# An attention bias table moved from the router's stage to the first projections

## The chip, the core and the metric

The kernel runs on one core of one Trainium2 chip. The metric is the device time of one execution in microseconds (us), as the median of several runs.

## What is computed

Two transformer blocks over 256 tokens of width 1024, all in f32. The first block projects x with one wide matrix and runs four token mixers on the result: A (RWKV-7), B (HGRN2), C (mLSTM) and D (RG-LRU). Their outputs are gated, merged, projected and added to x (layer norm 1); then come a mixture of 32 experts with the top 4 per token, and a gated embedding ("ple"). The second block has attention in three dilated windows and a pooling mixer. Its attention adds a relative position bias:

```python
dist = BLOCK + i - j
bucket = t5_bucket(jnp.clip(dist, 0, n_back) * dil)
bias = jnp.transpose(bias_g[bucket].astype(jnp.float32), (2, 0, 1))
logits = jnp.where(mask[None, :, None], logits + bias[None, None], -jnp.inf)
```

There are 24 heads (3 groups of 8), and the bias of a head depends on the distance of query and key alone.

## The kernel before

The kernel is written by hand, one instruction stream for each engine, with semaphores between them. SBUF is one tensor, `arena`, cut by offsets into named rooms, so that rooms of different stages overlap; PSUM is four banks `proj` and four banks `small`. Each product that goes through a `small` bank has a name in the list SMALL (L130 to L154), and the n-th uses bank n % 4: TensorE waits until VectorE has emptied the product four places ahead (`small`, L611), and VectorE takes them in the same order (`full`, L1581). PROJ and the `proj` banks work alike, with ScalarE emptying them (`out`, L1340).

SyncE (L500) streams the weights. The list UNITS (L111) has one entry for each 2 MB of weights, in the order in which TensorE uses them: "D xr", "D gate", "C q", "C k", "C if" (32 KB), "C v", "C o", "B f", ... They go through a ring of three rooms, so the load of unit n is issued when unit n-3 has been used (L504, L510). Behind the last of them SyncE loads the weights of expert 0 (L515 to L518, six units), then runs a loop over the experts in which each unit is loaded again as soon as TensorE has used it (L521 to L529), and then UNITS2 for the second block.

TensorE (L599) transposes x (L658), multiplies the first half of "D xr" (L667), transposes the packed vectors (L670), and goes on with "D xr", "D gate", "C q" (`ones_channels`, matmul at L627), the gates of D (L681), "C k", "C if" (L688), "C v" (`ones_tokens`, L637), "C o" and so on. The mixers' own chains come between projections. The end of the first block is `mixed` (L1039), `x1_turned` (L1049), `logits` (L1058), `ada_rows` (L820), `ada` (L828), then "ple" (L1102) and "pp" (L1143); the expert loop has L1176 (gate and up) and L1208 (down).

VectorE ends that stage with `residual` (L2002), `centred` (L1991 to L1993) and `normed` (L1997) for each of the two token tiles. Between the two calls for the second tile ScalarE computes a reciprocal root (`rsqrt`, L1407 and L1408). `normed` signals `x1_done`, for which `x1_turned` on TensorE waits.

The bias table is made of three small inputs: `rel_bias_2` (32 buckets x 24 heads), `hot` (32 x 384, each column the bucket of one distance) and `mask` (24 x 384). GpSimd loads them (L575 to L577) after the second merge. TensorE multiplies RELB by HOT behind the last `mixed` (L1066, L1067), VectorE adds the mask between `centred` and `normed` of the second tile (L2021 to L2023), and ScalarE stores the 24 x 384 result 128 times over into DRAM (L1470, L1471: 3072 rows of 1536 bytes, 4.7 MB). SyncE reads it back with a slanted access pattern (L535 to L538), which turns it into the bias for every query, in the second block. The buffers RELB, HOT, BM and TAB lie among the router's and the modulation's small tensors (L362 to L368).

At the start GpSimd loads two gate biases (L548, L549), clears WX and WAD (L550, L551), loads the blocks of D's gates into them (L555), and three matrices of A (L557 to L559). VectorE copies XT (L1607) and the vectors (L1608), then computes a small chain of lru_lambda together with ScalarE (L1616 to L1625, L1368, L1370), then the convolutions (L1630, L1632). ScalarE empties "D xr", "D gate" and "C q" and then does the sigmoids of D's gates (L1376, L1377); much later, when the last of B's projections is out, it computes the sigmoid of qB into the room tB (L1418).

## Time and profile before

| | before |
|---|---|
| median of 3 runs | 1945.26 us (1944.66 to 1947.16) |
| profiled execution, its own time | 1947.88 us |
| its span, first to last instruction | 1945.7 us |
| TensorE busy | 1835.1 us (94%) |
| VectorE busy | 553.8 us (28%) |
| ScalarE busy | 237.2 us (12%) |
| GpSimd busy | 43.9 us (2%) |
| mean granted TensorE clock | 0.975 of full speed |
| DMA | 537.69 MB, mean 276 GB/s |

The span in 40 equal slices of 48.6 us; a digit is a share in tenths, 9 is 90% or more:

```profile
PE   8999998899999999999999999999999979999998
PEld 7688886699865344333333333333333327768984
DVE  3543486555234211111111111111111130014412
ACT  0322122000100001100101101101101111011100
POOL 1000000130000000000000000000000000000000
PEclk9999998899898999999999999999999989999999
DMA  7443342512138899999999999999999975532331
GB/s 258 147 156 124 105 140 87 189 72 90 47 122 299 351 422 428 428 428 428 429 428 428 428 428 428 429 428 429 427 429 427 429 287 195 165 130 87 103 135 60
```

The first 12 slices are the projections and mixers of the first block up to layer norm 1, the 13th and 14th are router, "ple" and the first expert, the 15th to the 32nd the expert loop, and the rest the second block. PE is TensorE's matmuls, PEld its weight loads, which overlap them. In the loop the DMA rate stands at 427 to 429 GB/s.

### The profile page before, as it was taken

How to read it: one execution, taken by the hardware profiler on the slowest of the kernel's cores; microseconds unless marked ns; L12 is line 12 of the kernel's file. 1: busy time of each engine (PE TensorE's matmuls, PEld its weight loads, DVE VectorE, ACT ScalarE, POOL GpSimd, SP SyncE). 2: the span in 40 equal slices, each digit the busy share in tenths (PEclk: the TensorE clock that was granted, in tenths of full speed). 3: DMA queues.
4: the chain of work that ended last, by engine and by line, in shares of the span. 5: the costliest groups of instructions: out<-in, count | busy, mean ns of one | idle time of the engine just before them, and what ended most of it. 6: DMA issues, size and time to landing. Idle time of an engine off the chain costs nothing. (4 is left out here: it accounts for less than half of the span.)

```text
span 1945.7 us, 21418 instructions
## 1 busy us (share of the span) xinstructions
PE 1835.1 (94%) x8829; PEld 1074.9 (55%) x8829; DVE 553.8 (28%) x1037; ACT 237.2 (12%) x379; POOL 43.9 (2%) x39
## 2 busy tenths in 40 slices
PE   8999998899999999999999999999999979999998
PEld 7688886699865344333333333333333327768984
DVE  3543486555234211111111111111111130014412
ACT  0322122000100001100101101101101111011100
POOL 1000000130000000000000000000000000000000
PEclk9999998899898999999999999999999989999999
DMA  7443342512138899999999999999999975532331
GB/s 258 147 156 124 105 140 87 189 72 90 47 122 299 351 422 428 428 428 428 429 428 428 428 428 428 429 428 429 427 429 427 429 287 195 165 130 87 103 135 60
DMA packets 94139, 537.69 MB, mean 276 GB/s; under 512 B 5763, under 2 KB 15277, under 8 KB 69385
## 3 DMA queue, kind: packets, MB, share of 16 engines
q1 hardware_dynamic: 88960, 527.53, 67.4%
q10 hardware_dynamic: 3464, 4.85, 0.9%
q0 software_dynamic: 1664, 4.58, 0.8%
q8 instruction: 38, 0.62, 0.1%
q14 instruction: 13, 0.10, 0.0%
HBM read 531.18 MB, written 5.77 MB: 276 GB/s over the span
## 5 line engine op out<-in xcount | busy, mean ns | idle before, releaser
L1176 PE MATMUL small<-arena 128*64 128x512 f32 x2048 | 459.7, 597 | 44.2 <-DMA arena<-in_expert_w_gu 44.2
L1176 PEld LDWEIGHTS small<-arena 128*64 128x64 f32 x2048 | 160.0, 137 | 338.3 <-issue 248.7
L1208 PE MATMUL small<-arena 128*64 128x512 f32 x1024 | 226.8, 594 | 4.6
L2119 DVE TENSOR_SCALAR arena<-small 128x512 f32<-128x512 f32 x32 | 22.1, 692 | 721.7 <-PE small L1183 721.7
L627 PE MATMUL proj<-arena 128*128 128x256 f32 x960 | 211.5, 381 | 0.0
L627 PEld LDWEIGHTS proj<-arena 128*128 128x128 f32 x960 | 182.6, 191 | 25.7 <-issue 1.0
L1229 PE MATMUL proj<-arena 128*128 128x256 f32 x768 | 167.5, 379 | 0.0
L1229 PEld LDWEIGHTS proj<-arena 128*128 128x128 f32 x768 | 145.4, 190 | 20.3 <-issue 1.0
L1208 PEld LDWEIGHTS small<-arena 128*64 128x64 f32 x1024 | 84.7, 137 | 124.6 <-issue 124.6
L1347 ACT ACTIVATE arena<-proj 128x512 f32<-128x512 f32 (+1 forms) x76 | 45.3, 597 | 542.5 <-PE proj L885 168.3
L1485 ACT ACTIVATE arena<-arena 128x512 f32<-128x512 f32 x32 | 20.2, 630 | 548.1 <-DVE arena L2119 548.1
L1158 PE MATMUL proj<-arena 64*128 64x512 f32 x264 | 65.6, 615 | 0.7 <-ACTq L1495 0.7
L1123 PE MATMUL small<-arena 128*64 128x512 f32 x264 | 63.9, 605 | 0.0
L1238 PE MATMUL proj<-arena 128*128 128x512 f32 x128 | 59.9, 626 | 3.9 <-DVE arena L2145 3.9
L885 PE MATMUL proj<-arena 128*128 128x256 f32 x256 | 63.0, 402 | 0.0
L885 PEld LDWEIGHTS proj<-arena 128*128 128x128 f32 x256 | 50.6, 203 | 7.5
L2176 DVE TENSOR_TENSOR arena<-proj,arena 128x512 f32<-128x512 f32 (+2 forms) x24 | 13.4, 558 | 124.2 <-PE proj L1272 123.7
L648 PE MATMUL small<-arena 128*128 128x256 f32 x192 | 45.5, 401 | 3.4 <-DVE arena L1964 3.4
L1158 PEld LDWEIGHTS proj<-arena 64*128 64x128 f32 x264 | 22.7, 186 | 43.1 <-issue 41.5
L1493 ACT ACTIVATE arena<-small 128x512 f32<-128x512 f32 x32 | 19.1, 597 | 212.3 <-PE small L1208 212.3
L1238 PEld LDWEIGHTS proj<-arena 128*128 128x128 f32 x128 | 25.6, 203 | 34.7 <-issue 30.1
L648 PEld LDWEIGHTS small<-arena 128*128 128x128 f32 x192 | 38.6, 202 | 9.5 <-DVE arena L1964 3.6
(445 smaller groups left out, 1634.2 us busy)
## 6 DMA issues: line engine op xcount, KB each, us to landing
arena<-in_expert_w_gu SPq DMA_DIRECT2D x128, 2048.0 KB, 24.7
arena<-in_expert_w_down SPq DMA_DIRECT2D x64, 2048.0 KB, 20.4
arena<-in_w_in_first SPq DMA_DIRECT2D x20, 2048.0 KB, 7.8
arena<-in_w_in SPq DMA_DIRECT2D x16, 2048.0 KB, 9.1
arena<-in_w_ada SPq DMA_DIRECT2D x6, 2048.0 KB, 7.9
arena<-in_w_branch SPq DMA_DIRECT2D x4, 2048.0 KB, 7.8
arena<-in_w_out SPq DMA_DIRECT2D x4, 2048.0 KB, 8.1
bias_rows<-arena ACTq DMA_DIRECT2D x1, 4608.0 KB
```

The lines of the kernel that those rows point to most:

```text
L627: mm = pe.matmul(ps[:, m * T:m * T + T], w[:, k, (2 * b + m) * P:(2 * b + m + 1) * P], XT[:, k, :], start=k == 0, stop=k == KD - 1)
L648: mm = pe.matmul(ps[:, m * T:m * T + T], w[:, k, (2 * i + m) * P:(2 * i + m + 1) * P], YT[b][:, k, :], start=k == 0, stop=k == KW - 1)
L885: mm = pe.matmul(ps[:, m * T:m * T + T], w[:, k, quarter * P:quarter * P + P], XT[:, k, :], start=k == 0, stop=k == KD - 1)
L1123: mm = pe.matmul(bank[CAP * half:CAP * half + CAP, :], PICK[:, j, :], x1[:, j, half * W:half * W + W], start=j == 0, stop=j == 1, skip_gro ...
L1158: mm = pe.matmul(acc_bank[2 * j + half][:, :], PTW[lo:lo + CAP, j * P:j * P + P], YSB[lo:lo + CAP, :], start=False, stop=False, skip_group ...
L1176: mm = pe.matmul(bank[CAP * half:CAP * half + CAP, :], XG[:, k % 4, k // 4, :], w[:, k % 2, n * D + half * W:n * D + half * W + W], start= ...
L1208: mm = pe.matmul(y_bank[CAP * half:CAP * half + CAP, :], HM[:, m, u, :], w[:, m, half * W:half * W + W], start=u == 0 and m == 0, stop=u = ...
L1229: mm = pe.matmul(ps[:, m * T:m * T + T], w[:, k, (2 * b + m) * P:(2 * b + m + 1) * P], HT[:, k, :], start=k == 0, stop=k == KD - 1)
L1238: mm = pe.matmul(ps[:, :], HT[:, k, j * P:j * P + P], w[:, k, :], start=k == 0, stop=k == KD - 1)
L1347: act.activation(dst, v, func).then_inc(sig("proj_out"), 1)
L1485: act.activation(SGH, GH, ACT.Sigmoid, scale=1.702).then_inc(sig("sig_ready"), 1)
L2119: TS(GH, gate_bank[:, :], 7.0, None, ALU.min).then_inc(sig("g_ready"), 1)
```

## The change

The three loads move to the start of GpSimd's stream; the matmul follows the transposition of the vectors on TensorE, and in SMALL "bias" now stands behind "vectors"; the add follows the copy of the vectors on VectorE; the store is issued by ScalarE behind the evictions of "C q". RELB, HOT and TAB lie in the room that branch B later uses as tB (HIGH + 9728), the mask is loaded into TAB itself and added in place, and ScalarE waits for the store before it writes tB. The small statistics of layer norm 2 and later move to another offset.

```diff
--- before.py
+++ after.py
@@ -127,7 +127,7 @@
             ([f"L {h + 1} {i}" for i in range(3)] if h < 7 else []) + [f"{('Z', 'U', 'ZP', 'g2a')[h // 2]} {h % 2}"]]
          + ["g2a 2", "g2a 3"] + [f"g2p {i}" for i in range(4)])
 
-SMALL = ([f"x {i}" for i in range(4)] + ["vectors"]
+SMALL = ([f"x {i}" for i in range(4)] + ["vectors", "bias"]
          + ["D gx 0", "D gx 1", "D ga 0", "D ga 1"]
          + ["C row 0", "C row 1", "C col"] + [f"C S {h}" for h in range(4)]
          + ["C num 0", "C num 1", "C den", "C yT 0", "C yT 1"]
@@ -146,7 +146,7 @@
          + ["A S 0", "A U 1 0", "A U 1 1", "A S 1", "A Y 0", "A Y 1", "A U 2 0", "A U 2 1", "A S 2", "A U 3 0", "A U 3 1"]
          + ["A Y 2", "A Y 3", "A yT 0", "A yT 1"]
          + [f"Wb A {i}" for i in range(4)] + ["mix 0", "mix 1", "mix 2", "x1 0 0", "x1 0 1", "mix 3"]
-         + ["bias", "logits 0", "ada rows 4", "x1 1 0", "x1 1 1", "logits 1", "pT", "ada rows 5", "ada 4", "ada 5", "gate8"]
+         + ["logits 0", "ada rows 4", "x1 1 0", "x1 1 1", "logits 1", "pT", "ada rows 5", "ada 4", "ada 5", "gate8"]
          + ["ple 0", "gateB 0", "gateB 1", "ple 1", "gateT", "rank", "ple 2", "ple 3", "picked", "pp 0", "pp 1", "xg", "pp 2", "pp 3"]
          + ["h 0", "h 1"]
          + [f"{n} {h}" + s_ for h in range(HEADS) for n, s_ in (("T", " 0"), ("T", " 1"), ("T", " 2"), ("O", ""))]
@@ -283,6 +283,9 @@
         tB2 = room(at, KW, T); at += 1024
         stB = room(at, 2, 8); at += 16
         fB0 = tB2
+        RELB = room(HIGH + 9728, 24)[0:32]
+        HOT = room(HIGH + 9728 + 24, BKT)[0:32]
+        TAB = room(HIGH + 9728 + 24 + BKT, BKT)[0:24]
         assert at <= HIGH + 3 * UNIT
 
 
@@ -359,14 +362,10 @@
         PV2 = room(at, 40); at += 40
         MODT = room(at, 24); at += 24
         G8 = room(at, P)[0:8]; at += P
-        RELB = room(at, 24)[0:32]; at += 24
-        HOT = room(at, BKT)[0:32]; at += BKT
         CB = room(at, KD, 32); at += KD * 32
         SEL = room(at, 1); at += 1
         assert at <= LOW - 3 * 1024
-        BM = room(at, BKT)[0:24]; at += BKT
-        TAB = room(at, BKT)[0:24]; at += BKT
-        assert at <= LOW - 2 * 1024
+        at = LOW - 2 * 1024 - 64
         st2 = room(at, 2, 12); mv2 = room(at + 24, 2, 2); rs2 = room(at + 28, 2); ss2 = room(at + 30, 2)
         rs3 = room(at + 32, 2); ss3 = room(at + 60, 2, 2)
         mod_a = room(at + 36, 8); den = room(at + 44, 2, 4); nmax = room(at + 52, 2, 4)
@@ -547,6 +546,8 @@
         def _(pool):
             pool.dma_start(ifb[0:4, 0:1], ins["mlstm_i_bias"].rearrange("a b -> b a")).then_inc(sig("ifb_loaded"), 16)
             pool.dma_start(ifb[0:4, 1:2], ins["mlstm_f_bias"].rearrange("a b -> b a")).then_inc(sig("ifb_loaded"), 16)
+            for dst, src in ((RELB, ins["rel_bias_2"]), (HOT, consts["hot"]), (TAB, consts["mask"])):
+                pool.dma_start(dst, src).then_inc(sig("table_loaded"), 16)
             pool.memset(WX, 0.0).then_inc(sig("wx_zero"), 1)
             pool.memset(WAD, 0.0).then_inc(sig("wx_zero"), 1)
             pool.wait_ge(sig("wx_zero"), 2)
@@ -572,9 +573,6 @@
                     pool.wait_ge(sig("small_full"), small_no(f"A X{l - 1} 3") + 1)
                 pool.tensor_tensor(NTm, NT, along(c("level", l * P, l * P + P), 16), ALU.mult).then_inc(sig("NTm_ready"), 1)
 
-            pool.wait_ge(sig("merged"), 2)
-            for dst, src in ((RELB, ins["rel_bias_2"]), (HOT, consts["hot"]), (BM, consts["mask"])):
-                pool.dma_start(dst, src).then_inc(sig("table_loaded"), 16)
             pool.wait_ge(sig("A_states_done"), 1)
             pool.wait_ge(sig("small_full"), small_no("A Y 3") + 1)
             pool.dma_start(bcg, ins["ln1_g"][0].partition_broadcast(P)).then_inc(sig("ln1_loaded"), 16)
@@ -668,6 +666,8 @@
             mm.then_inc(sig("proj_full"), 1)
             pe.wait_ge(sig("prow_loaded"), 16 * len(VEC))
             pe.transpose(small("vectors")[:, 0:NVEC], PROW[0:NVEC, :], ident[0:NVEC, 0:NVEC]).then_inc(sig("small_full"), 1)
+            pe.wait_ge(sig("table_loaded"), 48)
+            pe.matmul(small("bias")[0:24, 0:BKT], RELB, HOT, start=True, stop=True).then_inc(sig("small_full"), 1)
             ones_channels("D xr", (1,))
             ones_channels("D gate")
             ones_channels("C q")
@@ -1063,8 +1063,6 @@
             mixed(1, 0)
             x1_turned(0)
             mixed(1, 1)
-            pe.wait_ge(sig("table_loaded"), 48)
-            pe.matmul(small("bias")[0:24, 0:BKT], RELB, HOT, start=True, stop=True).then_inc(sig("small_full"), 1)
             logits(0)
             ada_rows(4)
             x1_turned(1)
@@ -1371,6 +1369,9 @@
             channels("D xr", xr[:, :, 3:])
             channels("D gate", lgate)
             channels("C q", cz[:, 0:4, 3:])
+            act.wait_ge(sig("table_done"), 1)
+            act.dma_start(scratch.rearrange("p h c -> h p c"), along(TAB, P)).then_inc(sig("table_stored"), 16)
+
 
             act.wait_ge(sig("D_gates"), 1)
             do(act.activation(gx, gx, ACT.Sigmoid), "D_sig")
@@ -1415,6 +1416,7 @@
                 out(f"B i {j}", vB[:, j, :])
             channels("B g", gB)
             act.wait_ge(sig("proj_out"), proj_no("B g 1") + 1)
+            act.wait_ge(sig("table_stored"), 16)
             do(act.activation(tB, qB, ACT.Sigmoid))
             do(act.activation(kB, fB0, ACT.Sigmoid, scale=-1.0))
             do(act.activation(eB, gB, ACT.Sigmoid), "B_sig")
@@ -1467,9 +1469,6 @@
             log_and_exp()
             for j in range(TT):
                 rsqrt(rs1[:, j:j + 1], "ln1_var", "ln1_rstd", j + 1)
-            act.wait_ge(sig("table_done"), 1)
-            act.dma_start(scratch.rearrange("p h c -> h p c"), along(TAB, P)).then_inc(sig("table_stored"), 16)
-
             act.wait_ge(sig("logits_ready"), 1)
             do(act.activation(ex, ex, ACT.Exp), "router_exp")
             for i in range(4):
@@ -1606,6 +1605,9 @@
             for g in range(4):
                 do(dve.tensor_copy(XT[:, 2 * g:2 * g + 2, :], tiles(full(f"x {g}"))), "small_out")
             do(dve.tensor_copy(PV[:, 0:NVEC], full("vectors")[:, 0:NVEC]), "small_out")
+            dve.wait_ge(sig("table_loaded"), 48)
+            do(TTn(TAB, full("bias")[0:24, 0:BKT], TAB, ALU.add), "small_out")
+            dve.nop().then_inc(sig("table_done"), 1)
 
 
             do(dve.memset(xr[:, :, 0:3], 0.0))
@@ -2018,9 +2020,6 @@
             x1_turned(0)
             residual(1, 1)
             centred(mixv, st1, mv1, rs1, bcg, 1, "ln1_var")
-            dve.wait_ge(sig("table_loaded"), 48)
-            do(TTn(TAB, full("bias")[0:24, 0:BKT], BM, ALU.add), "small_out")
-            dve.nop().then_inc(sig("table_done"), 1)
             normed(x1, mixv, rs1, bcb, 1, "ln1_rstd", "x1_done")
             logits(0)
             ada_rows(4)
```

## Rows read from the trace of the kernel before

**Rows 1.** Waits of TensorE, 660 to 1640 us: us in total, times, longest.
```profile
PE small L1176 <- DMA arena<-in_expert_w_gu: 44.2, 51, 1.3
```

**Rows 2.** Busy time by stretch: us, PE PEld DVE ACT POOL, PEclk, DMA share, GB/s.
```profile
660.00:670.00 10.00, 10.00 (x40) 3.13 (x38) 0.57 (x3) 0.00 (x0) 0.00 (x0) 0.79 0.75 275
670.00:680.00 10.00, 10.00 (x50) 2.92 (x46) 2.77 (x5) 0.63 (x1) 0.00 (x0) 1.00 1.02 436
```

**Rows 3.** Time line of SyncE: start us, us, what.
```profile
665.52 0.35 SPq L529 DMA_DIRECT2D arena<-in_expert_w_gu  x1
```

**Rows 4.** Busy time by stretch again, two of the first 60 of 10 us.
```profile
20.00:30.00 10.00, 10.00 (x49) 8.76 (x48) 3.21 (x15) 1.61 (x4) 0.00 (x0) 1.00 1.06 409
200.00:210.00 10.00, 10.00 (x52) 8.85 (x51) 2.70 (x7) 1.88 (x2) 0.00 (x0) 1.00 0.59 211
```

**Rows 5.** Waits of TensorE, 0 to 600 us.
```profile
PE small L828 <- DVE arena L1814: 4.0, 1, 4.0
```

**Rows 6.** Time line around the old place of the bias table.
```profile
591.47 0.82 PE L1067 MATMUL small<-arena 32*24 32x384 f32 x2
592.22 1.97 PE L1058 MATMUL small<-arena 128*128 128x32 f32 x16
593.83 0.20 ACT L1408 ACTIVATE arena<-arena 128x1 f32<-128x1 f32 x1
594.86 0.55 DVE L2022 TENSOR_TENSOR arena<-small,arena 24x384 f32<-24x384 f32 x1
595.55 0.33 ACTq L1471 DMA_DIRECT2D bias_rows<-arena  x1
595.56 1.28 DVE L1997 SCALAR_TENSOR_TENSOR arena<-arena 128x1024 f32<-128x1024 f32 x1 [0.16 <-DVE arena L2022]
596.90 1.09 PE L1049 MATMUL small<-arena 128*128 128x128 f32 x8 [0.85 <-DVE arena L1997]
```

**Rows 7.** Busy time by stretch, two of 5 us behind the old place.
```profile
600.00:605.00 5.00, 5.00 (x26) 3.77 (x29) 1.76 (x8) 0.00 (x0) 0.00 (x0) 0.50 0.73 199
610.00:615.00 5.00, 4.68 (x12) 2.79 (x12) 0.61 (x3) 0.00 (x0) 0.00 (x0) 0.50 0.96 235
```

**Rows 8.** DMA issues, us to landing last, three stretches: 604:612, 620:622, 0:120.
```profile
arena<-in_ple_gate_w SPq DMA_DIRECT2D x1, 2048.0 KB, 18.2
...
arena<-in_expert_w_gu SPq DMA_DIRECT2D x1, 2048.0 KB, 27.0
...
arena<-in_rwkv_g POOLq DMA_DIRECT2D x1, 256.0 KB, 9.1
```

**Rows 9.** Waits of TensorE, 590 to 700 us.
```profile
PE small L828 <- DVE arena L1814: 1.7, 1, 1.7
```

**Rows 10.** Time line around the new place of the matmul.
```profile
20.53 0.27 PE L670 MATMUL small<-arena 126*128 126x126 f32 x1
...
27.75 0.60 ACT L1347 ACTIVATE arena<-proj 128x512 f32<-128x512 f32 x1 [4.62 <-PE proj L627]
```

**Rows 11.** Time line of the first 12 us, three rows.
```profile
1.91 0.54 POOL L549 DMA_DIRECT2D arena<-in_mlstm_f_bias  x1
...
10.30 0.69 DVE L1607 COPY arena<-small 128x512 f32<-128x512 f32 x1 [0.16 <-PE small L658]
11.39 2.04 PE L667 MATMUL proj<-arena 128*128 128x256 f32 x4 [1.19 <-DMA arena<-in_w_in_first]
```

**Rows 12.** Time line of 55 to 94 us, around the store's new place.
```profile
55.37 0.37 SPq L510 DMA_DIRECT2D arena<-in_w_in_first  x1
...
59.68 1.06 ACT L1376 ACTIVATE arena<-arena 128x1024 f32<-128x1024 f32 x1 [2.41 <-DVEq L1645]
...
72.63 0.37 SPq L510 DMA_DIRECT2D arena<-in_w_in_first  x1
...
79.53 14.00 PE L637 MATMUL proj<-arena 128*128 128x512 f32 x32
93.37 27.79 PE L627 MATMUL proj<-arena 128*128 128x256 f32 x128
```

## The prediction

> **What bounds the kernel now.** I read the waits of TensorE over the expert loop first, then the stretches around the loop's start, then the time lines of the two places that the change touches. In the expert loop TensorE's one large wait is for the gate and up weights, 44.2 us in 51 waits [rows 1], and from 670 us on the DMA engines are busy throughout (share 1.02, 436 GB/s, [rows 2]). So the loop is bound by the stream of weights. The stream's start is not: between 660 and 670 us the DMA share is only 0.75 [rows 2], because expert 0 fills the ring ahead of time and the first reload waits until TensorE has used a unit of it. SyncE issues that reload at 665.5 us [rows 3]. Whatever moves TensorE before 665.5 us moves the stream, and with it the end, by as much; what moves a transfer alone before that moves nothing, unless TensorE comes to wait for it.
>
> Before 665.5 us TensorE is the chain. From 20 to 210 us it is busy without a gap (first and last of 19 stretches of 10 us, all with 10.00 us busy, [rows 4]). From there to 590 us it waits now and then for VectorE or GpSimd, 4.0 us in the longest wait [rows 5], and those chains start from TensorE's own products, so that a delay of TensorE early on passes through them.
>
> **The old place, TensorE and VectorE.** The table's matmul starts at 591.47 us and the router's first logits matmul at 592.22: it takes 0.75 us of TensorE's issue [rows 6]. But TensorE waits a little later, 0.85 us, for L1997, the last step of the second layer norm tile, before it transposes that tile (L1049) [rows 6]. So what counts is when L1997 is done. On VectorE the table's add L2022 stands ahead of it: the add starts at 594.86 us, L1997 at 595.56. ScalarE's reciprocal root was ready at 593.83 + 0.20 = 594.03 [rows 6], so without the add L1997 can start where the add did, 595.56 - 594.86 = **0.70 us earlier**. What is late next is again VectorE, with the copies of x1, and then the second logits: the same order as before, with TensorE 0.75 us earlier in front of it, so all of it moves by 0.70. After that the top-4 chain on VectorE, the row copy for "ada 5", TensorE's waits at L828 for it (1.7 us, [rows 9]) and the "ple" units follow one another without slack up to 665.5 us. Term: **-0.70 us**. Ends: 0, if something that I don't see holds the copies back; and -1.05, because from 600 to 605 us the granted clock is at 0.50, the level of 1.2 GHz [rows 7], and 0.70 us more of the second logits would run at 2.4 GHz before it falls, which saves half of that, 0.35.
>
> **The old place, transfers.** The store (L1471) is an issue of 0.33 us on ScalarE [rows 6], which then has nothing to do until the router's exponential: 0. Its traffic is not small. With it the DMA share is 0.73 at only 199 GB/s between 600 and 605 us [rows 7], the second "ple" unit needs 18.2 us to land and an expert unit 27.0 us [rows 8]. But that "ple" unit is issued when "ada 4" is used, near 608 us, and wanted some 23 us later; expert 0 is wanted only behind "pp", the experts' biases and more; in the list of TensorE's waits between 590 and 700 us the longest is for VectorE, 1.7 us, and none is for a DMA [rows 9]. So taking the traffic away is worth **0**, under the cover of TensorE's own work. GpSimd's three loads, which stand between merge C and a wait for branch A's states, keep nobody waiting: 0.
>
> **The new place, TensorE.** The matmul goes in behind the transposition of the vectors (L670) and ahead of the second half of "D xr" (L627), where TensorE does nothing but issue. It costs its issue time. The nearest row is the same matmul in the old place, 0.75 us from its start to the next one's [rows 6]. Ends: 0.27 us, which the transposition of 126 columns takes [rows 10], and 0.82 us, the busy time of the table's own [rows 6]. I take **+0.75 us**. All of it lasts, for TensorE is busy without a gap for 190 us more. The Trainium skill, page "TensorE: Matmul & The Clock Gate", section "Back-to-back issue gap", gives N/2.4 + 2.5 ns for one pass at the full clock; four passes of 384 columns would be 0.65 us (an estimate, the number of passes is mine), and by it the sum below would be 0.10 us lower.
>
> **The new place, the loads.** GpSimd issues the three loads behind the two of the gate biases, of which the second takes 0.54 us and ends at 2.45 us [rows 11]; loads of its queue land in 9.1 us at most [rows 8]. So the last, issued by 4.1, is there by some 13 us, and TensorE asks at 20.8: 0. On GpSimd the two memsets, the loads of lru_wx and lru_wa and those behind them move back by 3 x 0.54 = 1.6 us; the first of them is wanted behind "C q 1", near 55 us: 0. One transfer does hold TensorE here, the first half of "D xr", 1.19 us until 11.39 [rows 11]. The three loads are 90 KB; ahead of it, at the 199 GB/s of the slowest stretch shown [rows 7], they are 0.45 us. On the other side 1.6 us of the lru traffic now come later, and TensorE could begin up to 0.3 us sooner, after VectorE's last copy (10.30 + 0.69, [rows 11]). I take 0, with -0.3 and +0.45 as ends.
>
> **The new place, VectorE and ScalarE.** VectorE waits for the matmul (done near 21.7 us) and adds for 0.55 us, so the lru_lambda chain behind it on both engines and ScalarE's first eviction come some 1.3 us later. ScalarE is idle for 4.62 us before its second eviction at 27.75 [rows 10], VectorE's convolutions wait for that eviction, and the bank of the first is wanted again only by "C q 0", near 41 us: 0. The store is issued behind "C q 1", where ScalarE then waits 2.41 us for VectorE [rows 12]: 0.33 us, hidden. The wait for the store ahead of the sigmoid of tB stands five units of weights further on, more than 90 us: 0. The traffic now meets the loads of "C v" (issued 55.37 us, wanted 79.53) and "C o" (issued 72.63, wanted 93.37) [rows 12]. With the 18.2 us of the "ple" unit they land at 73.6 and 90.8, both in time: 0.
>
> **Sum.** +0.75 - 0.70 = **+0.05 us**, between -1.1 (0.27 - 0.3 - 1.05) and +1.3 (0.82 + 0.45 - 0). The profiled execution took 1947.88 us, 2.2 us around its span of 1945.7; it lies 2.6 us above the median of the three runs shown, 1945.26 (1944.66 to 1947.16). The difference is put on the median: **1945.3 us**.
>
> **Rivals.**
> - The store stalls TensorE (0.04). Its traffic moves from under work that had no use for the DMA to where each unit is wanted soon. It decides at "C o": if that load takes more than 93.37 - 72.63 = 20.7 us, TensorE stands. With the slowest landing under the store, 27.0 us [rows 8], the wait is 6.3 us and the time 1951.6. Against it: the unit of the 27.0 us had others ahead of it in its queue, "C o" has none.
> - The clock (0.13). The stretches 600 to 605 and 610 to 615 us lie wholly at 0.50 [rows 7]. Such a low stretch is some 6.5 us long, so one more or one less is worth up to half, 3.2 us. The work there is thin: short waits, matmuls of 32 columns. If the shift of 0.7 us lets one go, 1942.0 (0.08); if it brings one, 1948.5 (0.05). By the Trainium skill, the same page, section "The HAM clock gate (the "warmup" mystery)", the gate follows how busy the engine has been of late, on a schedule that does not start with the kernel; by that rule a matmul taken out of a thin stretch speaks against this change, which is the 1948.5; the trace agrees in that both stretches follow waits of TensorE. For a shift that does nothing: four executions of the kernel lie within 3.2 us, each begun at another moment.
> - Half of the change is swallowed (0.06): one of TensorE's waits between 210 and 590 us takes up the 0.75 us, and the 0.70 stay: 1944.6. Against it: those waits hang on TensorE's own products.
>
> **How the numbers follow.** My forecast has 0.77. A measurement of this kernel can tell about 0.2% from no change, 3.9 us: below 1941.4 or above 1949.2. Faster, 0.05: a low stretch gone together with the lower end of the other terms, or two gone. Slower, 0.05: the store's 0.04 and 0.01 of the clock. Same, 0.90. The range takes in one low stretch either way and the ends of the sum, 1942.0 to 1948.5.
>
> **What would show it.** Right: the table's matmul near 21 us and the next projection 0.75 us behind; no DMA wait of TensorE for "C v" or "C o", with the DMA share near 1 behind 56 us; L1997's successor right behind L1993; the expert units ahead of the loop landing faster, to nobody's use; the first reload within 1 us of 665.5. Wrong: a DMA wait of TensorE between 76 and 110 us, ScalarE held at the store's issue, another number of low stretches before 665 us.

## The result, and the profile of the changed kernel

| | before | after |
|---|---|---|
| median, 20 runs each on one chip | 1944.6 us (1942.18 to 1947.33) | 1948.24 us (1939.38 to 1951.19) |
| ratio, 95% interval | | 1.0015 (1.0008 to 1.0021) |
| profiled execution / its span | 1947.88 / 1945.7 us | 1947.88 / 1945.7 us |

The change costs 0.15%, 2.9 us by the ratio. That is inside the 0.2% that was called no change, though the end of the interval, 1.0021, passes that bound. The forecast was 1945.3 us, with a range from 1942.0 to 1948.5; the median lies 0.3 us under the upper end. The two profiled executions took the same time to the hundredth, so the cost is not to be found by setting one profile against the other. It is found over all runs, further down. The profiles do show what became of each step. The page first, in the order of busy times, slices of TensorE, granted clock, DMA and rate:

```profile
PE 1835.3 (94%) x8829; PEld 1077.5 (55%) x8829; DVE 553.7 (28%) x1037; ACT 237.2 (12%) x379; POOL 44.0 (2%) x39
...
PE   8999998899998999999999999999999979999998
...
PEclk9999999799898999999999999999999999999999
DMA  7743333521236799999999999999999975542331
GB/s 260 238 157 111 111 120 107 184 87 53 79 125 253 295 420 428 429 428 429 428 429 428 429 428 429 428 429 428 429 428 429 428 290 199 167 130 87 103 134 61
```

The store's 4.7 MB now lie in the second slice (238 GB/s; it was 147), and the 13th and 14th carry less (253 and 295; they were 299 and 351). The clock's low digit has moved as well.

**The first microseconds**, time line of GpSimd, VectorE and TensorE (start, duration, engine, line, operation; in brackets the idle time before it and what ended it):

```profile
2.44 0.53 POOL L550 DMA_DIRECT2D arena<-in_rel_bias  x1
...
3.47 0.52 POOL L550 DMA_DIRECT2D arena<-shape_mask  x1
...
10.05 0.69 DVE L1606 COPY arena<-small 128x512 f32<-128x512 f32 x1 [0.16 <-PE small L656]
...
10.80 9.46 PE L665 MATMUL proj<-arena 128*128 128x256 f32 x32 [0.85 <-DVE arena L1606]
...
20.09 0.27 PE L668 MATMUL small<-arena 126*128 126x126 f32 x1
...
20.30 0.82 PE L670 MATMUL small<-arena 32*24 32x384 f32 x2
...
21.05 10.20 PE L625 MATMUL proj<-arena 128*128 128x256 f32 x46
21.25 0.55 DVE L1609 TENSOR_TENSOR arena<-small,arena 24x384 f32<-24x384 f32 x1 [0.49 <-PE small L670]
...
28.26 0.60 ACT L1345 ACTIVATE arena<-proj 128x512 f32<-128x512 f32 x1 [4.42 <-PE proj L625]
```

TensorE starts "D xr" at 10.80 us instead of 11.39 [rows 11], and behind VectorE's copy instead of a transfer. The table's matmul takes 0.75 us of issue, 20.30 to 21.05, as in the old place. VectorE's add is there at 21.25, and ScalarE still has 4.42 us to spare ahead of its second eviction.

**The store and the units that it meets**, time line of ScalarE, SyncE and TensorE, then the list of DMA issues (KB each, us to landing) for "C v" and "C o":

```profile
55.89 0.37 ACTq L1373 DMA_DIRECT2D bias_rows<-arena  x1
...
60.19 1.06 ACT L1377 ACTIVATE arena<-arena 128x1024 f32<-128x1024 f32 x1 [2.41 <-DVEq L1647]
...
73.14 0.37 SPq L509 DMA_DIRECT2D arena<-in_w_in_first  x1
...
80.05 14.00 PE L635 MATMUL proj<-arena 128*128 128x512 f32 x32
93.88 6.42 PE L625 MATMUL proj<-arena 128*128 128x256 f32 x29
```

```profile
arena<-in_w_in_first SPq DMA_DIRECT2D x1, 2048.0 KB, 12.9
...
arena<-in_w_in_first SPq DMA_DIRECT2D x1, 2048.0 KB, 19.2
```

"C o" was issued at 73.14 us, landed 19.2 us later at 92.3, and was wanted at 93.88: a margin of 1.5 us. In a4_store_late, the experiment below that has no store here, the same two loads landed in 7.7 and 7.9 us. Neither unit makes TensorE wait; the rows of their matmuls, at 80.05 and 93.88, have no idle time before them.

**The old place**, time line of TensorE and VectorE, and TensorE's waits from 590 to 700 us (idle us, times, mean):

```profile
595.75 0.69 DVE L2004 SCALAR_TENSOR_TENSOR arena<-arena,small 128x512 f32<-128x512 f32 x1 [4.87 <-PE small L1039]
...
598.96 1.28 DVE L1999 SCALAR_TENSOR_TENSOR arena<-arena 128x1024 f32<-128x1024 f32 x1
...
600.30 0.88 PE L1049 MATMUL small<-arena 128*128 128x128 f32 x6 [1.10 <-DVE arena L1999]
```

```profile
PE small L828 <- DVE arena L1816: 2.0, 1, 2.0
...
PE small L1049 <- DVE arena L1999: 1.1, 1, 1.1
```

No wait is for a DMA, and the longest is the one for VectorE at L828, 2.0 us, before 1.7 [rows 9]. From the residual L2004 to L1999, the last step of the layer norm, it is 598.96 - 595.75 = 3.21 us. Before, it was 3.90 (L2002 at 591.66, L1997 at 595.56). The add's 0.69 us have gone from VectorE's path. But this profile reaches the place 4.1 us late: the residual is at 595.75 instead of 591.66.

**Where the 4.1 us were lost, and got back.** The stretches of the changed kernel (length, TensorE busy, weight load, VectorE, ScalarE, GpSimd, granted clock, DMA share, GB/s), and those of the kernel before:

```profile
120.00:130.00 10.00, 10.00 (x41) 8.20 (x40) 3.68 (x10) 2.58 (x3) 0.00 (x0) 0.83 0.60 210
220.00:230.00 10.00, 6.18 (x29) 5.63 (x28) 5.59 (x9) 1.06 (x1) 1.53 (x3) 0.68 0.61 212
655.00:660.00 5.00, 5.00 (x13) 2.07 (x12) 3.14 (x5) 0.00 (x0) 0.00 (x0) 1.00 0.38 98
660.00:665.00 5.00, 5.00 (x21) 1.67 (x21) 2.51 (x6) 0.00 (x0) 1.08 (x2) 1.00 0.90 374
```

```profile
120.00:130.00 10.00, 10.00 (x50) 8.48 (x49) 3.68 (x10) 3.10 (x3) 0.00 (x0) 1.00 0.61 210
220.00:230.00 10.00, 7.59 (x43) 6.92 (x44) 7.35 (x12) 1.06 (x1) 0.00 (x0) 1.00 0.41 153
655.00:660.00 5.00, 5.00 (x12) 1.48 (x12) 3.45 (x5) 0.00 (x0) 1.07 (x2) 0.75 0.88 305
660.00:665.00 5.00, 5.00 (x16) 1.44 (x14) 0.57 (x3) 0.00 (x0) 0.00 (x0) 0.57 0.80 324
```

In the clock records the changed kernel has two low stretches, of 3.4 us from 124.9 and of 6.8 us from 223.9, where the kernel before has none. The kernel before has one of 6.8 us from 657.5, ahead of the loop, where this profile of the changed kernel has none. So SyncE's issues, 4.1 us late at the first "ple" unit (595.67 us instead of 591.57), are level again at the first reload of the loop, 665.62 us against 665.52 [rows 3]:

```profile
665.62 0.35 SPq L528 DMA_DIRECT2D arena<-in_expert_w_gu  x1
```

From the reload on the time is the same (665.62 to the end: 1280.08 us, before 1280.18). The loop's wait for weights is 44.5 us; it was 44.2 [rows 1].

Two single profiles do not show that the edit made the stretches at 125 and 224 us. The kernel of the experiment a3_late_removed, below, is the kernel before up to 590 us, and its profile has them too:

```profile
120.00:130.00 10.00, 10.00 (x42) 8.14 (x41) 3.80 (x11) 3.48 (x4) 0.00 (x0) 0.83 0.60 210
220.00:230.00 10.00, 6.31 (x24) 5.81 (x25) 5.83 (x9) 1.06 (x1) 0.76 (x2) 0.66 0.53 198
```

**All executions.** Each execution comes with its span and its mean granted clock c. The low level is 1.2 GHz, 0.50 of the full 2.4. So span x (1 - c) is the time lost to it if TensorE sets the pace throughout, and span x c is what the program would then take at full clock; call it the work. The clock is given to three digits, up to 1 us in one execution, but the means are good to some 0.5 us. Over 103 executions of the kernel before (those beside the experiments below) and all others, means with standard errors:

| kernel | work, us | lost to low clock, us | executions with c of 0.974 or less |
|---|---|---|---|
| before | 1897.65 ± 0.17 | 44.9 ± 0.2 | 0 of 103 |
| after | 1896.7 ± 0.4 | 48.7 ± 0.8 | 10 of 20 |
| a1_loads_only | 1896.6 ± 0.5 | 44.3 | 0 of 11 |
| a2_early_doubled | 1898.15 ± 0.4 | 45.4 | 0 of 11 |
| a3_late_removed | 1896.7 ± 0.4 | 45.4 | 0 of 11 |
| a4_store_late | 1896.1 ± 0.3 | 49.4 ± 1.1 | 7 of 11 |
| b1_spread_after | 1899.8 ± 0.5 | 46.2 | 0 of 11 |
| b2_spread_before | 1901.5 ± 0.4 | 43.4 | 0 of 12 |
| b3_more_work | 1897.6 ± 0.3 | 46.7 | 0 of 11 |
| b4_fill | 1903.4 ± 0.3 | 40.6 | 0 of 11 |
| c1_split_after | 1899.2 ± 0.4 | 45.0 | 0 of 12 |
| c2_split_loads_only | 1898.2 ± 0.35 | 42.9 | 0 of 12 |
| c3_loads_behind | 1896.6 ± 0.5 | 50.0 ± 0.9 | 8 of 12 |
| c4_before_more | 1898.0 ± 0.3 | 43.6 | 0 of 11 |

By this split the change makes the work 0.9 us less and the loss 3.8 us more, together the 2.9 us of the ratio. Half of its executions lie lower in the clock than any of the kernel before: those ten took 1949.7 us in the mean, the other ten 1945.4. The profiled one, c = 0.976, is of the second kind.

The split is rough, because low time in which TensorE waits costs nothing. At the end of the loop before's profile has 17.1 us of low clock (from 1592.8 us), the changed kernel's 13.7 (from 1596.1). The split books 1.7 us of loss for that, and the two profiles take the same time from the reload to the end within 0.1 us; TensorE stands idle there until 1600.07 us, for 9.4 us at a stretch, and the 3.4 us more lie in that idle time. Within the kernels (259 executions, each against the mean of its kernel) 0.001 less of c goes with 1.35 us more span, not 1.95, and the rounding of c explains only some 0.1 of the difference. So, as an estimate, about a quarter of what is booked as loss is none, and the column of work is too small by as much. By this estimate the 3.8 us of loss cost 2.9, all of the change's price, and its work is level. Differences of less than 1 us in the column of work are not to be read.

The bound of 0.974 is no sharp one either. Counted at 0.975 or less it is 5 of 103 for before, 11 of 20 for after, 7 of 11 for a4, 11 of 12 for c3, 4 of 11 for b1, 3 of 12 for c1, 1 of 11 each for a1, a2 and a3, and none for the rest.

### The profile page after: what moved, and what is told of

Read it like the earlier page. It is cut to its first block and busy times, and to the rows that moved or that the text cites. A ratio compares the mean times of both kernels' runs of the same rounds, so it can differ in the third digit from the quotient of the medians.

```text
span 1945.7 us, 21420 instructions
## 1 busy us (share of the span) xinstructions
PE 1835.3 (94%) x8829; PEld 1077.5 (55%) x8829; DVE 553.7 (28%) x1037; ACT 237.2 (12%) x379; POOL 44.0 (2%) x39
## 5 line engine op out<-in xcount | busy, mean ns | idle before, releaser
L1174 PE MATMUL small<-arena 128*64 128x512 f32 x2048 | 457.3, 595 | 44.5 <-DMA arena<-in_expert_w_gu 44.5
L1156 PE MATMUL proj<-arena 64*128 64x512 f32 x264 | 65.6, 615 | 0.7 <-ACTq L1494 0.7
L1121 PE MATMUL small<-arena 128*64 128x512 f32 x264 | 63.9, 605 | 0.0
L885 PE MATMUL proj<-arena 128*128 128x256 f32 x256 | 62.4, 400 | 0.0
```

The costliest lines, as they stand in the source:

```text
L885: mm = pe.matmul(ps[:, m * T:m * T + T], w[:, k, quarter * P:quarter * P + P], XT[:, k, :], start=k == 0, stop=k == KD - 1)
L1121: mm = pe.matmul(bank[CAP * half:CAP * half + CAP, :], PICK[:, j, :], x1[:, j, half * W:half * W + W], start=j == 0, stop=j == 1, skip_gro ...
L1156: mm = pe.matmul(acc_bank[2 * j + half][:, :], PTW[lo:lo + CAP, j * P:j * P + P], YSB[lo:lo + CAP, :], start=False, stop=False, skip_group ...
L1174: mm = pe.matmul(bank[CAP * half:CAP * half + CAP, :], XG[:, k % 4, k // 4, :], w[:, k % 2, n * D + half * W:n * D + half * W + W], start= ...
```

## The experiments

Each was timed against the kernel before on one chip. Two accounts of the extra time were tried against each other: that it is the clock, falling once more in some executions because of where TensorE's work stands, and that it is real work or waiting that the moved loads, matmul or store bring.

| kernel | median, us (range), runs | ratio to before (95%) |
|---|---|---|
| a1_loads_only | 1942.67 (1941.26 to 1945.29), 11 | 0.9992 (0.9983 to 1.0001) |
| a2_early_doubled | 1945.73 (1941.86 to 1948.26), 11 | 1.0005 (0.9996 to 1.0014) |
| a3_late_removed | 1943.95 (1941.81 to 1946.35), 11 | 0.9995 (0.9986 to 1.0004) |
| a4_store_late | 1948.49 (1941.45 to 1951.16), 11 | 1.0016 (1.0004 to 1.0027) |
| b1_spread_after | 1948.73 (1942.88 to 1951.3), 11 | 1.0014 (1.0005 to 1.0023) |
| b2_spread_before | 1947.7 (1942.7 to 1950.46), 12 | 1.0012 (1.0003 to 1.0021) |
| b3_more_work | 1946.26 (1945.09 to 1947.97), 11 | 1.0008 (1.0 to 1.0017) |
| b4_fill | 1946.7 (1942.53 to 1948.66), 11 | 1.0008 (0.9999 to 1.0017) |
| c1_split_after | 1946.94 (1939.54 to 1950.43), 12 | 1.0008 (0.9997 to 1.0019) |
| c2_split_loads_only | 1942.68 (1940.88 to 1946.33), 12 | 0.9996 (0.9987 to 1.0004) |
| c3_loads_behind | 1948.94 (1943.43 to 1950.87), 12 | 1.0023 (1.0014 to 1.0031) |
| c4_before_more | 1942.98 (1941.66 to 1946.9), 11 | 0.9997 (0.9988 to 1.0006) |

Medians of before beside them: 1944.69 (33 runs, a), 1944.51 (35, b), 1944.46 (35, c). The three groups ran on three chips, and the changed kernel was not timed again beside them. Where a run is set against the changed kernel's 20, the comparison goes by way of the kernel before, whose medians agree within 0.25 us.

### The parts alone

**a1_loads_only**: the kernel before, and the three loads early as well, into rooms of their own.

```diff
+            for dst, src in ((RELE, ins["rel_bias_2"]), (HOTE, consts["hot"]), (TABE, consts["mask"])):
+                pool.dma_start(dst, src).then_inc(sig("early_loaded"), 16)
             pool.memset(WX, 0.0).then_inc(sig("wx_zero"), 1)
```

> The kernel before, with the three small loads issued early a second time into branch B's room, where nobody reads them; matmul, add and store stay at the old place. In the changed kernel TensorE's first projection began 0.43 us sooner than before. Theory LOADS (the reordered GpSimd queue does that): the same here, and the time within 1 us of before. Theory CLOCK (the +3 us of the change is low-clock time that a small shift of TensorE's early work brings): a shift of -0.4 us can by itself move the time by 1 to 3 us, and the time follows the mean granted clock of each run. Theory STORE (the store's traffic among the early loads costs the time): no change against before.

It came out 2.0 us under the kernel before, more than an account without gain allowed, though the interval of the ratio still reaches 1.0001. By the table it is work, -1.0 us, and 0.6 us less loss, neither of them clear by itself. The profile shows the transfer's wait gone:

```profile
11.01 8.95 PE L672 MATMUL proj<-arena 128*128 128x256 f32 x32 [0.85 <-DVE arena L1613]
```

Instead of waiting for the DMA until 11.39 us [rows 11], TensorE starts at 11.01, behind VectorE. In all nine profiles with the small loads at the front of GpSimd's stream TensorE starts between 10.62 and 11.04 us, in the five without between 11.39 and 11.84. That the larger lru loads, pushed back by them, are what "D xr" competed with is the reading that fits; it was not measured by itself.

**a2_early_doubled**: a1 with the early matmul and add as well; the old place keeps its own.

```diff
-SMALL = ([f"x {i}" for i in range(4)] + ["vectors"]
+SMALL = ([f"x {i}" for i in range(4)] + ["vectors", "bias0"]
...
+            pe.wait_ge(sig("early_loaded"), 48)
+            pe.matmul(small("bias0")[0:24, 0:BKT], RELE, HOTE, start=True, stop=True).then_inc(sig("small_full"), 1)
...
+            dve.wait_ge(sig("early_loaded"), 48)
+            do(TTn(TABE, full("bias0")[0:24, 0:BKT], TABE, ALU.add), "small_out")
```

> The kernel before, with loads, matmul and add at the new place into a room that nobody reads, and the whole old place kept, the store too. Theory CLOCK: the early shift alone brings the loss, so +0.75 us of work and about 2 to 3 us of low clock, 3 to 4 us over before. Theory STORE: +0.75 us only. Theory SUM (my prediction's terms and nothing else): +0.75 us, at most 1.

The work is 1.5 ± 0.6 us above a1's, where 0.75 was the price of the matmul: the right sign, and the size is off by little more than one error. No execution has the low clock of the changed kernel. The account by the clock, 3 to 4 us over before from the early part alone, missed: by the ratio it is 1.0 us.

**a3_late_removed**: the kernel before without the late matmul and add; the store writes the mask alone.

```diff
-            pe.wait_ge(sig("table_loaded"), 48)
-            pe.matmul(small("bias")[0:24, 0:BKT], RELB, HOT, start=True, stop=True).then_inc(sig("small_full"), 1)
...
-            do(TTn(TAB, full("bias")[0:24, 0:BKT], BM, ALU.add), "small_out")
-            dve.nop().then_inc(sig("table_done"), 1)
...
-            act.dma_start(scratch.rearrange("p h c -> h p c"), along(TAB, P)).then_inc(sig("table_stored"), 16)
+            act.dma_start(scratch.rearrange("p h c -> h p c"), along(BM, P)).then_inc(sig("table_stored"), 16)
```

> The kernel before, without the table's matmul and add at the old place, nothing at the new one; the store stays at the old place and stores the mask alone. The product of the relative bias is left out. Theory SUM: -0.7 us. Theory CLOCK: -0.7 us plus or minus one low stretch behind the place, -4 to +3, with the start of the kernel as before. Theory STORE: -0.7 us.

Work 0.9 ± 0.5 us less; the term was 0.70. Again no execution at 0.974 or less. So neither part alone brings the loss.

**a4_store_late**: the changed kernel with a store of the same size, of the mask alone, put back behind the layer norm.

```diff
-            act.wait_ge(sig("table_done"), 1)
-            act.dma_start(scratch.rearrange("p h c -> h p c"), along(TAB, P)).then_inc(sig("table_stored"), 16)
...
+            act.wait_ge(sig("mask_loaded"), 16)
+            act.dma_start(scratch.rearrange("p h c -> h p c"), along(BM, P)).then_inc(sig("table_stored"), 16)
             act.wait_ge(sig("logits_ready"), 1)
```

> The changed kernel with the store put back behind the layer norm, from a room into which the mask alone is loaded; the matmul and the add stay early. The product is left out of what is stored. Theory STORE: the loss of 3 us goes, the time is that of before within 1 us. Theory CLOCK: it stays, 2 to 4 us over before.

1948.49 us, like the changed kernel, with work, loss and share of executions (7 of 11 against 10 of 20) the same within their errors. The store's place is not the cause. Its profile also shows the extra fall. Time line of TensorE around the start of the loop, and the stretches there:

```profile
656.90 4.37 PE L1151 MATMUL proj<-arena 32*128 32x512 f32 x8
661.21 16.62 PE L1177 MATMUL small<-arena 128*64 128x512 f32 x64
```

```profile
655.00:660.00 5.00, 5.00 (x12) 1.97 (x11) 3.55 (x3) 0.00 (x0) 0.00 (x0) 0.98 0.59 184
660.00:665.00 5.00, 5.00 (x12) 1.24 (x12) 1.32 (x6) 0.00 (x0) 1.08 (x2) 0.50 0.94 395
665.00:670.00 5.00, 5.00 (x22) 1.52 (x20) 0.00 (x0) 0.00 (x0) 0.00 (x0) 0.84 0.67 198
```

TensorE is busy without a gap, from 656.90 us on with eight matmuls (32 rows, 512 columns) that set up the experts' biases, and the clock is low for 6.8 us from 660.1. Expert 0's 64 matmuls then take 16.62 us. In the changed kernel's profile, without a low stretch there, they take 13.95:

```profile
658.09 3.69 PE L1148 MATMUL proj<-arena 32*128 32x512 f32 x8
661.72 13.95 PE L1174 MATMUL small<-arena 128*64 128x512 f32 x64
```

This profiled execution is the only one of the fourteen kernels' that has c at 0.974 or less (0.973). So it is the one view of which stretch a slower execution has more. Granted clock of stretches of 20 us, where the profiles differ most, and the low time between 100 and 700 us worked out from them (twice the missing share of each stretch):

| profile | 120 | 220 | 640 | 660 | low, us |
|---|---|---|---|---|---|
| before | 1.00 | 1.00 | 0.94 | 0.89 | 68.4 |
| after | 0.91 | 0.83 | 1.00 | 1.00 | 68.8 |
| a2, a3, b1, b3, c1, c3 | 0.91 | 0.83 | 1.00 | 1.00 | 68.4 to 68.8 |
| a4 | 0.91 | 0.83 | 0.99 | 0.83 | 76.0 |
| b2 | 1.00 | 0.83 | 1.00 | 1.00 | 65.6 |
| a1, c4 | 0.91 | 0.91 | 1.00 | 1.00 | 62.4 |
| c2 | 1.00 | 0.88 | 1.00 | 1.00 | 65.2 |
| b4 | 0.91 | 0.91 | 1.00 | 1.00 | 52.0 |

(The stretches from 160, 300 to 380, 500 to 560 and 600 us are low in part in nearly all of them, and are in the last column too.) Before's profile has the low stretch ahead of the loop and not those at 125 and 224 us; most others have these and not that; a4's has both, and 7.2 to 7.6 us more low time than the profiles of before and after. Half of it would be 3.6 to 3.8 us; the block and expert 0's matmuls together took (4.37 - 3.69) + (16.62 - 13.95) = 3.35 us longer than in the changed kernel's profile. At the end of the loop a4's has 3.4 us of low time more as well (17.1 us from 1595.4), as before's has, which is part of its low c. The stretch of 3.4 us at 123 to 125 us and one at 222 to 224 stand in the profile of c4 too, whose kernel is the kernel before up to some 640 us. So where the stretches lie differs between profiles for another reason than the edit.

### The block of 32 rows, and more work

**b1_spread_after** and **b2_spread_before**: in the changed kernel and in that of before, the block is cut up, one of its four products behind each product of "pp".

```diff
                 mm.then_inc(sig("small_full"), 1)
+                pe.matmul(acc_bank[2 * j + half][:, :], GTT[:, j * P:j * P + P], BD[:, half * W:half * W + W], start=True, stop=False, skip_group_check=True)
...
-            for j in range(TT):
-                for half in range(2):
-                    pe.matmul(acc_bank[2 * j + half][:, :], GTT[:, j * P:j * P + P], BD[:, half * W:half * W + W], start=True, stop=False, skip_group_check=True)
```

> The changed kernel with the four matmuls of 32 rows that start the accumulators ahead of the expert loop (the line with GTT and BD) no longer in one block behind the last pp product but one behind each of the four. Same work. In profiles of the kernel before and of the changed kernel with the store put back, the granted clock falls to 0.50 at the end of that block and stays there for 6.8 us into the first expert; in those of the changed kernel itself and of the doubled early part it doesn't, and these executions are some 3 us shorter. Theory CLOCK: the fall at that place goes for good, the median is 2 to 3 us under the changed kernel's 1948.2 and the spread over the executions smaller. Theory WORK (the change adds 3 us of waits or work): no difference against the changed kernel, 1948.

> The same edit on the kernel before. Theory CLOCK: before had the fall at that place in few executions only, so little is won, 0 to 1 us, and the gap between the two kernels shrinks from 3.6 us to 1 us or less. Theory WORK: the gap stays at 3 us.

The loss is 46.2 ± 0.8 us in b1 against 48.7 ± 0.8, and no execution of 11 is at 0.974 or less, though four are at 0.975. But the edit costs work: 3.1 us in b1 and 3.9 in b2. The account by the clock, which expected 2 to 3 us under the changed kernel, missed. One piece of it can be read in b1's time line:

```profile
661.79 1.12 PE L1144 MATMUL proj<-arena 32*128 32x512 f32 x2
663.88 13.95 PE L1171 MATMUL small<-arena 128*64 128x512 f32 x64 [0.97 <-issue]
```

From L1121 at 648.63 us to the loop's first matmul it takes 15.2 us, where the changed kernel takes 13.0 (648.69 to 661.72). The medians, 1948.73 and 1947.7, are 1.0 us apart instead of the 3.6 of the kernels that they were made of. The edit takes away most of the difference between them, but it brings both near the level of the slower one.

**b3_more_work** puts one matmul of 128 rows and 512 columns, used by nobody, in front of the "picked" gather of the changed kernel; **c4_before_more** does the same to the kernel before.

```diff
+            pe.wait_ge(sig("proj_out"), proj_no("G A 3") + 1)
+            pe.matmul(acc_bank[0][:, :], ident, CO[:, 0:W], start=True, stop=True)
             pe.wait_ge(sig("pick_ready"), 1)
```

> The changed kernel with 0.86 us of extra TensorE work, one matmul of 128x512 that nobody reads, ahead of the first expert's gather, where TensorE is the chain. Theory WORK: 0.9 us slower than the changed kernel, 1949.1. Theory CLOCK: the place of the 32-row block moves by 0.86 us and with it how often the clock falls there; the doubled early part, which reaches this place some 0.7 us later than the changed kernel, was faster than it by 2.5 us, so here 1945.5 to 1947, with more work in less time.

> The kernel before with the 0.86 us of extra TensorE work ahead of the first expert's gather that took 2 us off the changed kernel. Theory WORK: +0.9 us against before, 1945.4. Theory CLOCK: here the fall ahead of the loop was rare and the shift can only make it more frequent or leave it, +0.9 to +3 us.

With more work the changed kernel did not get slower: 0.9 us more of it, 2.1 us less lost, 1946.26 us, and in the mean 1.1 ± 0.8 us less time. All eleven executions have c = 0.976, and they spread over 2.9 us instead of 11.8. An account by work alone asks for 0.9 us more and is off by 2.0 ± 0.8. But c4 missed: with the same matmul the kernel before came out at 1942.98, 1.5 us under its own median instead of above it (0.6 by the ratio, whose interval takes in 1), with 1.3 ± 0.6 us less lost and the work hardly up (+0.35). The loss moves by 1 to 2 us, each time some two errors, through edits whose own price is less than 1.

**b4_fill**: b1 with five such matmuls of 256 or 512 columns put into TensorE's thin stretches at the logits and the modulation.

```diff
+            def busy(n, cols):
+                for _ in range(n):
+                    pe.matmul(acc_bank[0][:, 0:cols], ident, CO[:, 0:cols], start=True, stop=True)
...
             ada_rows(4)
+            busy(1, 256)
             x1_turned(1)
+            busy(1, 512)
             logits(1)
...
             ada_rows(5)
+            busy(3, 512)
             ada(4)
```

> The changed kernel with the spread accumulator matmuls and with matmuls that nobody reads in three waits of TensorE behind the layer norm: 256 columns ahead of the transpositions of the second tile, 512 ahead of its logits, 3 x 512 ahead of ada 4. Theory CLOCK: with TensorE busy through these waits one or both of the low stretches between 599 and 617 us go, each worth up to 3.4 us: 1940 to 1944. Theory WORK: nothing gained or up to 1 us lost against the spread version.

The stretches of b4, and of the changed kernel:

```profile
600.00:610.00 10.00, 8.89 (x43) 4.61 (x36) 5.80 (x23) 0.26 (x1) 0.00 (x0) 0.87 0.38 134
610.00:620.00 10.00, 10.00 (x34) 5.15 (x33) 2.07 (x3) 1.91 (x2) 0.00 (x0) 0.96 1.04 425
```

```profile
600.00:610.00 10.00, 8.14 (x44) 5.59 (x44) 5.38 (x19) 0.26 (x1) 0.00 (x0) 0.66 0.27 104
610.00:620.00 10.00, 7.71 (x27) 4.86 (x24) 3.66 (x13) 0.00 (x0) 0.00 (x0) 0.66 0.78 281
```

Where TensorE stands less, the clock stays up: 0.87 and 0.96 instead of 0.66 and 0.66. Behind the layer norm one stretch of 3.4 us is left of two of 6.8. Over all runs 8.1 us less are lost than in the changed kernel, and 6.7 us more work done: 1946.7 us. Against b1, which has the same spread block, it is 5.5 us less lost for 3.6 us more work. The expectation by the clock, 1940 to 1944, missed by what the fillers and the spread block cost.

**c1_split_after** and **c2_split_loads_only** look for a split without b1's price: of the block's four products, two go behind "ple 2" and "ple 3" and two stay (c1 from the changed kernel, c2 from a1).

```diff
+                    if half == 1:
+                        if j == 0:
+                            pe.wait_ge(sig("small_out"), small_no("gateT") + 1)
+                        started(0, j)
...
-            for j in range(TT):
-                for half in range(2):
-                    pe.matmul(acc_bank[2 * j + half][:, :], GTT[:, j * P:j * P + P], BD[:, half * W:half * W + W], start=True, stop=False, skip_group_check=True)
+            for half in range(2):
+                started(1, half)
```

> The changed kernel with two of the four 32-row matmuls that start the accumulators moved up, one behind each of the products ple 2 and ple 3, so that the block ahead of the expert loop is half as long and still covers VectorE's work on the last pp product (the spread version lost 1.0 us there and about as much between its matmuls). Theory CLOCK: no fall of the clock ahead of the loop and no more than 0.3 us of cost, 1944.5 to 1946.5, that is 2 to 3.5 us under the changed kernel. Theory WORK: 1948 to 1949.

> The version with the early loads alone, which was the fastest so far (1942.67, 2 us under before), with the same split. Theory CLOCK: it had the fall ahead of the loop in few executions, so -0.5 to +0.3 us, 1942 to 1943, below both kernels. Theory WORK: 1942.7 to 1943.

c1 loses 3.7 ± 1.2 us less than the changed kernel and works 2.5 us more: 1946.94, a little above what was expected. c2 is at 1942.68, no better than a1, since the split again costs what it saves.

**c3_loads_behind**: the changed kernel with the three loads behind those of lru_wx and lru_wa.

```diff
-            for dst, src in ((RELB, ins["rel_bias_2"]), (HOT, consts["hot"]), (TAB, consts["mask"])):
-                pool.dma_start(dst, src).then_inc(sig("table_loaded"), 16)
             pool.memset(WX, 0.0).then_inc(sig("wx_zero"), 1)
...
+            for dst, src in ((RELB, ins["rel_bias_2"]), (HOT, consts["hot"]), (TAB, consts["mask"])):
+                pool.dma_start(dst, src).then_inc(sig("table_loaded"), 16)
             pool.dma_start(WA2[0:64, :], ins["rwkv_w2"][0])
```

> The changed kernel with GpSimd's three loads behind those of lru_wx and lru_wa instead of ahead of them. If the changed order of GpSimd's loads is what let TensorE begin at 11.0 instead of 11.4 us, it begins at 11.4 or later here, waiting for the first half of D xr. Theory SUM: 0.4 to 0.7 us over the changed kernel, 1948.9. Theory CLOCK: the work without the low clock is 0.4 to 0.7 us more than the changed kernel's, the time itself anywhere between 1944.5 and 1950, by the share of executions with low stretches.

```profile
11.84 1.39 PE L665 MATMUL proj<-arena 128*128 128x256 f32 x4 [2.25 <-DMA arena<-in_w_in_first]
```

The transfer's wait is back, 2.25 us of it, and TensorE starts at 11.84 instead of 10.80. So where these loads stand among GpSimd's does set the start. The work over all runs does not show the 1.0 us, though (1896.6 against 1896.7, each ± 0.5). The extra loss stays: 8 of 12 executions at 0.974 or less, 1948.94 us. Part of it has another source here: this profile's clock records have a low stretch of 3.4 us from 12.7 us, beside the wait for the transfer, that no other profile's records show. It counts for 1.7 us of the 50.0, and 48.3 would still be 3.4 above before.

## Why the prediction was right, and where it was not

"No change" was right, and the path and most terms were as worked out. That the time lies in the stated range is luck in part: the forecast was 2.9 us too low, nearly all of it the clock, and the range held because its upper end was the rival of one low stretch more, which had been given 0.05.

**The bound**: right. In the profiles of all 14 kernels the end lies 1279.3 to 1282.6 us behind the first reload, wherever between 659.2 and 667.8 us that is. The first four expert units landed sooner (median 14.5 us instead of 23.5) and served nobody. That this profile's reload at 665.62 us was within 1 us of 665.5, one of the signs of being right, is chance: those of a1 and c4 have it at 661.4 and 661.1.

**New place, TensorE** (+0.75): 20.30 to 21.05 us, +0.75. The estimate from the Trainium skill, page "TensorE: Matmul & The Clock Gate", section "Back-to-back issue gap", 0.65, is not borne out; its number of passes was a guess.

**Old place** (-0.70): the path from the residual to L1999 is shorter by 0.69 us. TensorE then waits 1.10 us for L1999, before 0.85, and the next steps follow as before.

**The start** (0, between -0.3 and +0.45): it measured 11.39 - 10.80 = 0.59 us of gain in the profiles, past the lower end. The two effects that were weighed against each other were the right ones, but the order of the loads outweighs the 90 KB by more than was thought. a1 and c3 show the step by itself, the one taking the wait away and the other bringing it back, and so do the ranges over all profiles, 10.62 to 11.04 us and 11.39 to 11.84; part of the gain in the changed kernel is VectorE's last copy, at 10.05 instead of 10.30 us. These three terms give 0.75 - 0.70 - 0.59 = -0.54 us; the mean of the work says -0.9 ± 0.4, or about nothing once a quarter of the loss is booked back. Neither is clear of the forecast's +0.05.

**The store** (0, a rival of 0.04): right, by 1.5 us. "C o" took 19.2 us of the 20.7 that it had, more than the 18.2 by which the place was judged, and "C v" 12.9. a4 shows no difference in time by the store's place. The sign "DMA share near 1 behind 56 us" did not come as stated: the share was 0.95, 0.76, 0.70 and 0.93 in the four stretches of 5 us from 60 us. With more than another 1.5 us on "C o" the store would have held TensorE up.

**The clock**: here the working failed. The forecast gave "a shift that does nothing" nearly all the weight, on the ground that four executions of the kernel before lie within 3.2 us, and the rival of one low stretch more, 1948.5 us, 0.05. That rival is what happened, as far as the runs show: half of the executions lie lower in the clock, 4.3 us above the other half, and in the mean +3.8 us of loss are booked. Its price was about right (half of 6.8 us is 3.4). What was wrong was the argument against it. That one program's executions agree says nothing of what another program's do. The place was not the one named either (600 to 620 us, where the clock is 0.66 in this kernel and 0.67 in the kernel before). The sign of being wrong, another number of low stretches before 665 us, did come (12 instead of 11), but it was no good sign: a3's profile has 12 as well, all but two of them ahead of its first changed instruction. The rule of the Trainium skill that the prediction cited, page "TensorE: Matmul & The Clock Gate", section "The HAM clock gate (the "warmup" mystery)", that the gate follows how busy the engine has been, agrees with b4 (0.87 and 0.96 instead of 0.66 and 0.66). As a reason for the 1948.5 it is not borne out: a3 takes just that matmul out of the thin stretch and loses 45.4 ± 0.6 us, before 44.9. Nor does it explain a4's fall at 660 us, where TensorE was busy throughout.

**What stays open.** Executions at 0.974 or less come in three kernels alone: after, a4 and c3. These have the early matmul, have not the late matmul and add, and keep the 32-row block whole and no filler. Of the kernels that lack one of these (a2 and a3, then b1, c1 and b3) or more, none has such an execution in 11 or 12. With the bound at 0.975, b1 and c1 are less clear. That they come from the stretch at 660 us on top of those at 125 and 224 rests on one profile, a4's; no slower execution of the changed kernel itself was profiled. How the edit makes them more frequent, and why they come in some executions and not in others, is not shown. The gains of work under 1 us are not settled one by one. No version beats the kernel before beyond its interval; a1 comes nearest, 0.9992 (0.9983 to 1.0001), by its early loads and by none of the moved work.

## What to carry to other kernels

Count the low clock as a term of its own: from each execution's span and mean granted clock it can be read over all runs, and it told here in a table what no pair of profiles showed. The figure is an upper bound, since low time under a wait costs nothing. In this kernel it is 45 us of 1945, and edits worth under 1 us of work went with shifts of 1 to 5. Where low stretches lie in one profile of each kernel says little: compare with a kernel that is the same up to that point. So an edit whose working sums to less than that is a change of the clock first, and only many runs tell its sign. A few small loads put ahead of larger ones on a free queue brought the first projection forward here, where TensorE had waited for a transfer: 10.62 to 11.04 us instead of 11.39 to 11.84.

## What the runs showed of the hardware

- The clock fell while TensorE was busy without a gap, in a block of matmuls with 32 rows and 512 columns: in a4 (block from 656.90, low from 660.1 us) and in the kernel before (block from 654.65, low from 657.5). In the changed kernel's profile the same block, from 658.09, passes at the full clock, as in six others that have it whole. So being busy without a gap did not keep the clock up, nor does the block always bring it down.
- Two kernels with the same work by the split (after and a3, 1896.7 both) lose 48.7 ± 0.8 and 45.4 ± 0.6 us to it.
- Low clock under a wait is free: 3.4 us more of it at the end of the loop, where TensorE stands idle for 9.4 us, changed the time behind the first reload by no more than 0.1 us (before and after).
- The store, 3072 rows of 1536 bytes, raised the landing of a 2 MB unit from 7.9 us (a4) to 19.2 in its new place, and its absence from the old place cut that of the second "ple" unit from 18.2 to 7.6.
